# Two products taken in pieces: the pieces put between two weight slabs instead of behind both

## The chip, the cores and the metric

The kernel runs on one core of a Trainium2 chip. The metric is the time of one execution on the device, in microseconds (us). The core has five engines with an instruction stream each: TensorE (matrix products), VectorE, ScalarE, GpSimd and SyncE, which here only issues transfers. They meet at semaphores: an instruction adds to one when it is done, and another engine waits until it has reached a value.

## The reference

Two layers of a decoder (width 2048) for 512 prompt tokens and 8 samples of 4 tokens, 544 columns in all. Only the beginning of the first layer matters here:

```
def ada_norm(x, c, ada_w, ada_b, norm_g):
    mod = jax.nn.silu(c) @ ada_w + ada_b
    shift, scale, gate = jnp.split(mod, 3, axis=-1)
    h = rms_norm(x, norm_g) * (1 + scale[:, None]) + shift[:, None]
    return h, gate[:, None]

def even_layer(...):
    h, gate = ada_norm(x, c, ada_w, ada_b, norm_g)
    qa, ka, va, ga, qb, kb, vb, gb, lr = split_cols(h @ w_in, EVEN_SPLITS)
    ...
```

`shift` and `scale` are products of 9 condition vectors (one of the prompt, 8 of the samples) with a weight of 2048 x 2048 each. `h` needs both, channel by channel. `h @ w_in` sums over all 2048 channels. Window attention and gated linear attention follow, an output projection, and a second layer with retention. Everything is in float32.

## The kernel before, in words

Activations lie with channels on the 128 partitions: 16 channel tiles of 128 x 544, numbered k. A product with a block of 128 weight columns is a sum over the 16 k. To keep float32 accuracy, weights and activations are split in a high and a low part (`W_hi`, `W_lo`, `act_hi`, `act_lo`, `WH`, `WL`, `AH`, `AL` in the code), and each k takes three matmuls (high x high, high x low, low x high) for each half of 272 columns. The first two blocks, keys (ka) and values (va) of the first layer, are the "first two products". They are kept in two accumulators at once, `PJ` and the first two banks of `X`.

The shift and scale weights come in eight pairs of slabs, i = 0 to 7. Slab 0 of pair i holds 256 shift columns and slab 1 the same 256 scale columns, 2 MB each (2048 KB). There is one buffer for each kind. So SyncE (L295, `ada_slabs`) issues the slab of pair i + 1 once the semaphore `ad_done` says that TensorE has multiplied the slab of pair i of the same kind.

TensorE multiplies a slab in `ada_slab` (L1498, the matmuls 128x256): slab 0 into bank `AD`, slab 1 into bank 4 of `X`. ScalarE copies the rows out (L627), `ada_slabs_select` (L1506) turns them back into columns, and VectorE adds the bias and writes `mod_even` (L1015). Then `first_norm` on VectorE and ScalarE makes the normed and modulated activations of the two channel tiles of this pair (ending with `act_lo`, L1039 and L1042); it tells of them by the semaphores `nl` and `nls0`.

`first_products(p)` on TensorE (L1537, matmuls 128x272) adds the two channel tiles of pair p to both products: 2 tiles x 2 products x 2 halves x 3 = 24 matmuls. It waits for the norm of pair p.

The order of the work is that in which the code of each engine is written; there is no scheduler. TensorE's loop goes over i = 1 to 7: both slabs of pair i, then the selects, then pieces of the products. From i = 3 on, the pieces of pair i - 1 stand behind the selects of pair i, and at i = 3 those of pairs 0 and 1 ahead of them, because the low part of the second weight block (semaphore `lo`) is there only then. `first_products(7)` stands behind the loop. When the products are complete, ScalarE copies them out (L598, L697) and splits the next weights (L594, `split_hi`), VectorE makes their low part (L992), and the third product begins (L1481).

GpSimd issues the other transfers. Two stores of the first residual (L386, 2176 KB each, all activations as loaded) wait for `ad_ev` 14, which is VectorE's last sum of pair 6. All transfers share the same 16 transfer engines; those of SyncE are in one queue (q1), those of GpSimd in another (q0).

Of the kernel before, what the change touches and what calls it, by code (L numbers as in the profile page):

```python
# [93 lines left out]
def build(nc, I, O, C):  # L94
    ctx = ExitStack()
    with ctx:
# [129 lines left out]
        s = {}  # L226
# [1232 lines left out]
        def _(pe):  # L1459
# [29 lines left out]
            def sum_rows(lhs, src, banks=(0, 1)):  # L1489
                for c in range(2):  # L1490
                    last = mm(X[:, banks[c], 0:HALF], lhs, src[:, c * HALF:(c + 1) * HALF], start=True, stop=True)  # L1491
                return last

            def ada_rows(w, bank):

                for k in range(KT):
                    g = 32 * (k % 4)
                    last = mm(bank[g:g + 32, 0:256], cs[:, 9 * k:9 * k + 32], w[:, k], start=(k < 4), stop=(k >= KT - 4),  # L1498
                              tile_position=(0, g))
                last.then_inc(s["ad_done"], 1)  # L1500
# [18 lines left out]
            def ada_slab(i, sl):  # L1519
                if i >= 1:  # L1520
                    pe.wait_ge(s["ad_ev"], 2 * i + sl - 1)
                pe.wait_ge(adl[sl], i * 16 + 16)
                ada_rows(slab[sl], AD if sl == 0 else X[:, 4])

            def ada_slabs_select(i):
                for sl in range(2):
                    ada_select(i * 2 + (sl + 1), arow0[:, sl], AD if sl == 0 else X[:, 4])

            def first_products(p):

                pe.wait_ge(s["nls0"], p + 1)
                for k in (2 * p, 2 * p + 1):
                    pe.wait_ge(s["nl"], k + 1)
                    for n, acc in ((0, PJ), (1, X)):
                        for c in range(2):
                            for a, (w, x) in enumerate(((WH, AH), (WH, AL), (WL, AH))):
                                last = mm(acc[:, c, 0:HALF], w[:, n, k], x[:, k, c * HALF:(c + 1) * HALF],  # L1537
                                          start=(k == 0 and a == 0), stop=(k == KT - 1 and a == 2))
                            if k == KT - 1:
                                last.then_inc(s["half"], 1)  # L1540
# [13 lines left out]
            ada_slabs_select(0)  # L1554
            for i in range(1, 8):
                ada_slab(i, 0)
                ada_slab(i, 1)
                ada_slabs_select(i)
                if i == 1:
                    pe.wait_ge(s["sqd"], KT + 1)  # L1560
                    sum_rows(ones[:, :], ssum).then_inc(s["ms"], 1)
                if i == 3:
                    pe.wait_ge(s["lo"], 2)
                    first_products(0)
                    first_products(1)
                if i >= 3:
                    first_products(i - 1)
            first_products(7)
            pe.wait_ge(s["vld2"], 16 * 6)
            pe.wait_ge(s["kv_rb"], 1)  # L1570
# [363 lines left out]
```

## Time and profile before

| | |
|---|---|
| median of 3 runs | 3147.58 us (3136.74 to 3150.88) |
| profiled execution | 3144.75 us, span 3142.8 us |
| mean granted clock of TensorE | 0.955 |
| TensorE busy | 2950.2 us (94% of the span) |
| VectorE, ScalarE, GpSimd busy | 1131.0, 922.9, 238.5 us |
| read from and written to memory | 370.36 and 72.51 MB |
| matmuls of L1481, three kinds of 5920 each | 293, 290 and 289 ns in the mean |

The span goes from the first to the last instruction of one execution; busy time is the time in which an engine had at least one instruction under way. Matmuls overlap, so that a matmul of 290 ns starts some 126 ns behind the one before it. Releasers are inferred: a row says for whom an engine waited by the profile.

### The profile page before, as it was taken

The page shows a single profiled execution, that of the slowest core. Times are in us where ns is not written, and L with a number is a line of the kernel's source. Part 1 is how long each engine was busy: PE and PEld are TensorE (multiplying, and loading weights), DVE is VectorE, ACT ScalarE, POOL GpSimd, SP SyncE. Part 2 cuts the span into 40 slices and gives each one's busy share as a digit, 9 for nine tenths or more (in the row PEclk, how much of TensorE's full clock was granted, in tenths as well). Part 3 has the DMA queues.
Part 4 walks back from the last instruction along what each step waited for, and adds up shares of the span by engine and source line. Part 5 has one row for each costly group of instructions (what it writes and reads, how often), then busy time and mean ns, then how long its engine had stood idle before and what let it go on. Part 6 is the DMA issues. An engine that isn't in the chain of part 4 may idle for free.

```text
span 3142.8 us, 53302 instructions
## 1 busy us (share of the span) xinstructions
PE 2950.2 (94%) x22444; PEld 2720.7 (87%) x22444; DVE 1131.0 (36%) x1628; ACT 922.9 (29%) x1346; POOL 238.5 (8%) x381
## 2 busy tenths in 40 slices
PE   4799997988989898999999999999999999899998
PEld 3688886977878897989989898989989898799998
DVE  4334442232232434433334343333434243433422
ACT  3244443232332322223223232322323232311221
POOL 1010000000000000001010100101010010110111
PEclk8899997988989898899999999999999999999999
DMA  9953332654645343325253443435343442655442
GB/s 319 325 160 115 113 114 75 183 150 151 187 147 163 105 138 100 116 85 168 85 174 105 135 133 109 154 89 167 95 152 115 128 152 81 198 166 168 116 136 64
DMA packets 525813, 442.86 MB, mean 141 GB/s; under 512 B 12255, under 2 KB 492021, under 8 KB 525056
## 3 DMA queue, kind: packets, MB, share of 16 engines
q1 hardware_dynamic: 485664, 300.30, 33.3%
q0 software_dynamic: 39808, 139.43, 12.6%
q8 instruction: 177, 2.90, 0.4%
q14 instruction: 20, 0.16, 0.0%
q10 hardware_dynamic: 144, 0.07, 0.0%
HBM read 370.36 MB, written 72.51 MB: 141 GB/s over the span
## 4 chain that ended last, share of the span: by engine, by line
PE 84%; DMA 5%; DVE 4%; ACT 4%; issue 3%; POOL 0%; ACTq 0%; DVEq 0%; SPq 0%; POOLq 0%
PE PJ L1481 66%; DMA W_raw<-in_ada_w_even 3%; PE X L1884 2%; PE X L1463 2%; PE AD L1498 2%; PE X L1878 2%; PE X L1851 1%; PE X L1835 1%; ACT W_hi L594 1%; PE X L1826 1%; DMA work<-in_state_gla 1%; PE X L1771 1%; PE X L1498 1%; PE X L1778 1%; PE X L1491 1%
## 5 line engine op out<-in xcount | busy, mean ns | idle before, releaser
L1481 PE MATMUL PJ<-act_hi,W_hi 128*128 128x272 f32 x5920 | 1736.1, 293 | 40.4 <-DVE act_lo L1299 22.4
L1481 PE MATMUL PJ<-act_lo,W_hi 128*128 128x272 f32 x5920 | 1713.9, 290 | 0.0
L1481 PE MATMUL PJ<-act_hi,W_lo 128*128 128x272 f32 x5920 | 1712.3, 289 | 0.0
L1481 PEld LDWEIGHTS PJ<-act_hi,W_hi 128*128 128x128 f32 x5920 | 1123.9, 190 | 86.5 <-issue 64.7
L1481 PEld LDWEIGHTS PJ<-act_lo,W_hi 128*128 128x128 f32 x5920 | 1124.4, 190 | 2.8
L1481 PEld LDWEIGHTS PJ<-act_hi,W_lo 128*128 128x128 f32 x5920 | 1121.6, 189 | 0.0
L992 DVE TENSOR_TENSOR W_lo<-W_raw,W_hi 128x2048 fp32r<-128x2048 f32 x185 | 423.8, 2291 | 522.8 <-ACT W_hi L594 516.2
L594 ACT ACTIVATE W_hi<-W_raw 128x2048 fp32r<-128x2048 f32 x185 | 352.9, 1908 | 263.7 <-PE PJ L1481 244.7
L598 ACT ACTIVATE tiles<-PJ 128x272 f32<-128x272 f32 (+1 forms) x224 | 88.9, 397 | 1029.1 <-PE PJ L1481 1028.5
L1381 DVE SCALAR_TENSOR_TENSOR W_raw<-W_raw,work,X 128x512 f32<-128x512 f32 x128 | 90.0, 745 | 143.7 <-PE X L1835 143.7
L1498 PE MATMUL AD<-W_raw,cs 128*32 128x256 f32 x1280 | 90.8, 432 | 17.9 <-DMA W_raw<-in_ada_w_even 13.1
L1498 PEld LDWEIGHTS AD<-W_raw,cs 128*32 128x32 f32 x1280 | 42.2, 122 | 54.7 <-issue 33.6
L598 ACT ACTIVATE work<-PJ 128x272 f32<-128x272 f32 x50 | 19.7, 395 | 210.6 <-PE PJ L1481 205.9
L515 POOL DMA_DIRECT2D out<-W_raw x64 | 46.5, 727 | 349.0 <-DVE W_raw L1381 344.8
L1331 DVE SCALAR_TENSOR_TENSOR work<-PJ,eps,work 128x240 f32<-128x240 f32 x32 | 15.0, 468 | 159.9 <-PE PJ L1481 159.9
L1884 PEld LDWEIGHTS X<-tiles,work 128*128 128x128 f32 x256 | 46.1, 190 | 30.0 <-issue 19.2
L1884 PE MATMUL X<-tiles,work 128*128 128x512 f32 (+3 forms) x256 | 71.7, 433 | 0.0
L1463 PE MATMUL X<-ident,tiles 128*128 128x128 f32 (+1 forms) x346 | 46.4, 283 | 23.4 <-DVE tiles L1176 13.5
L1463 PEld LDWEIGHTS X<-ident,tiles 128*128 128x128 f32 (+1 forms) x346 | 38.0, 139 | 27.8 <-DVE tiles L1176 15.1
L454 POOL DMA_DIRECT2D work<-resid x48 | 26.1, 544 | 438.7 <-DVE work L1335 246.0
L1371 DVE TENSOR_TENSOR tiles<-tiles,work 128x544 f32<-128x544 f32 x32 | 23.2, 724 | 92.4 <-ACT work L610 92.4
L1878 PE MATMUL X<-work 128*128 128x512 f32 x128 | 56.2, 592 | 0.0
(341 smaller groups left out, 2159.0 us busy)
## 6 DMA issues: line engine op xcount, KB each, us to landing
W_raw<-in_w_in_odd SPq DMA_DIRECT2D x96, 1024.0 KB, 5.8
W_raw<-in_ada_w_even SPq DMA_DIRECT2D x24, 2048.0 KB, 9.7
W_raw<-in_ada_w_odd SPq DMA_DIRECT2D x24, 2048.0 KB, 8.4
W_raw<-in_w_in_even SPq DMA_DIRECT2D x40, 1024.0 KB, 11.0
W_raw<-in_state_ret POOLq DMA_DIRECT2D x64, 512.0 KB, 6.6
out<-W_raw POOLq DMA_DIRECT2D x64, 512.0 KB, 3.2
W_raw<-in_w_out_odd SPq DMA_DIRECT2D x32, 1024.0 KB, 5.9
W_raw<-in_w_out_even SPq DMA_DIRECT2D x16, 1024.0 KB, 5.8
```

The source lines that it names most:

```text
L515: pool.dma_start(O[9][0][b, ds(h, 1)].rearrange("h (k p) e -> p (h k) e", p=128), SB[:, b % 4]).then_inc(sst[b % 4], 16)
L594: A(WH[:, par], first_raw if isinstance(n, int) and n < 2 else slot[par], ACT.Copy).then_inc(s["hi"], 1)
L598: return A(dst, PJ[0:rows, c, 0:HALF], ACT.Copy).then_inc(s["ev"], 1)
L992: TT(WL[:, par], raw_w, WH[:, par].bitcast(F32), ALU.subtract).then_inc(s["lo"], 1)
L1381: STT(SB[:, b % 4, kk], SB[:, b % 4, kk], RT[:, T + NS + NB + 4:T + NS + NB + 5], X[:, kk, :], ALU.mult, ALU.add).then_inc(s["c_upv"], 1)
L1463: return nc.tensor.transpose(out, in_, ident[0:rows, 0:rows])
L1481: last = mm(PJ[:, c, 0:HALF], w[:, par, k], x[:, k, c * HALF:(c + 1) * HALF], start=(k == 0 and a == 0), stop=(k == KT - 1 and a == 2))
L1491: last = mm(X[:, banks[c], 0:HALF], lhs, src[:, c * HALF:(c + 1) * HALF], start=True, stop=True)
L1498: last = mm(bank[g:g + 32, 0:256], cs[:, 9 * k:9 * k + 32], w[:, k], start=(k < 4), stop=(k >= KT - 4), tile_position=(0, g))
L1771: last = mm(X[:, 4, NS * e + NQ * b:NS * e + NQ * b + NQ], ST[:, b, ec], BP[:, 0, SEQ + NQ * b:SEQ + NQ * b + NQ], start=False, stop=(b == ...
L1878: last = mm(X[:, kk, :], KTK[:, t, 128 * kk:128 * kk + 128], CT[:, t], start=(t == 0), stop=(t == 3))
L1884: last = mm(X[:, 2 + e % 2, 128 * t:SEQ], CT[:, t, 128 * e:128 * e + 128], RAT[:, RAOFF[t]:RAOFF[t] + SEQ - 128 * t], start=(t == 0), stop ...
```

## The change

In TensorE's loop the pieces are moved. From i = 4 on, the pieces of pair i - 1 stand between slab 0 and slab 1 of pair i. The pieces of pairs 0 to 2, which stood behind the selects of pair 3, go to the same place at i = 4, ahead of those of pair 3, together with their wait for `lo`. Only `first_products(7)` stays behind the last selects. No other engine's code is touched.

```diff
--- before.py
+++ after.py
@@ -1554,17 +1554,17 @@
             ada_slabs_select(0)
             for i in range(1, 8):
                 ada_slab(i, 0)
+                if i == 4:
+                    pe.wait_ge(s["lo"], 2)
+                    for p in range(3):
+                        first_products(p)
+                if i >= 4:
+                    first_products(i - 1)
                 ada_slab(i, 1)
                 ada_slabs_select(i)
                 if i == 1:
                     pe.wait_ge(s["sqd"], KT + 1)
                     sum_rows(ones[:, :], ssum).then_inc(s["ms"], 1)
-                if i == 3:
-                    pe.wait_ge(s["lo"], 2)
-                    first_products(0)
-                    first_products(1)
-                if i >= 3:
-                    first_products(i - 1)
             first_products(7)
             pe.wait_ge(s["vld2"], 16 * 6)
             pe.wait_ge(s["kv_rb"], 1)
```

On TensorE, behind the last select of pair 3 (`AD` and `X` with `cs` are slab products, with `sel` selects, `PJ` with `act` and `W` the first piece):

```order
 L1506 MATMUL AD<-sel,work 128x9 x2
 L1506 MATMUL X<-sel,work 128x9 x2
+L1498 MATMUL AD<-W_raw,cs 32x256 x16
 L1537 MATMUL PJ<-act_hi,W_hi 128x272
 L1537 MATMUL PJ<-act_lo,W_hi 128x272
```

The product of slab 0 of pair 4 now stands ahead of the first piece.

On TensorE, between the pieces of pair 2 and those of pair 3:

```order
 L1537 MATMUL X<-act_lo,W_hi 128x272
 L1537 MATMUL X<-act_hi,W_lo 128x272
-L1498 MATMUL AD<-W_raw,cs 32x256 x16
-L1498 MATMUL X<-W_raw,cs 32x256 x16
-L1506 MATMUL AD<-sel,work 128x9 x2
-L1506 MATMUL X<-sel,work 128x9 x2
 L1537 MATMUL PJ<-act_hi,W_hi 128x272
 L1537 MATMUL PJ<-act_lo,W_hi 128x272
```

The slabs and selects of pair 4 are gone from here, so that four calls, 96 matmuls, stand in one row.

On TensorE, between the pieces of pair 6 and those of pair 7:

```order
 L1537 MATMUL X<-act_lo,W_hi 128x272
 L1537 MATMUL X<-act_hi,W_lo 128x272
+L1498 MATMUL X<-W_raw,cs 32x256 x16
+L1506 MATMUL AD<-sel,work 128x9 x2
+L1506 MATMUL X<-sel,work 128x9 x2
 L1537 MATMUL PJ<-act_hi,W_hi 128x272
 L1537 MATMUL PJ<-act_lo,W_hi 128x272
```

Slab 1 of pair 7 and the selects now stand ahead of the last 24 pieces alone.

## Rows read from the trace of the kernel before

**Rows 1.** the page: span, clock in 40 slices, chain that ended last
```profile
span 3142.8 us, 53302 instructions
...
PEclk8899997988989898899999999999999999999999
...
PE 84%; DMA 5%; DVE 4%; ACT 4%; issue 3%; POOL 0%; ACTq 0%; DVEq 0%; SPq 0%; POOLq 0%
```

**Rows 2.** chain of waits in order of time: start, duration, what
```profile
94.44 12.74 DMA W_raw<-in_ada_w_even
...
110.93 9.08 DMA W_raw<-in_ada_w_even
...
122.96 13.92 DMA W_raw<-in_ada_w_even
...
150.23 0.78 ACT work L598 x2
...
152.26 1.81 ACT W_hi L594
...
156.44 12.31 PE PJ L1481 x96
```

**Rows 3.** timeline of TensorE: start, duration, engine, line, what [idle time before]
```profile
81.02 0.61 PE L1506 MATMUL X<-sel,work 128*128 128x9 f32 x4
...
81.70 0.29 PE L1537 MATMUL PJ<-act_lo,W_hi 128*128 128x272 f32 x1
...
90.50 0.29 PE L1537 MATMUL X<-act_hi,W_lo 128*128 128x272 f32 x1
...
101.29 3.26 PE L1498 MATMUL AD<-W_raw,cs 128*32 128x256 f32 x32 [2.67 <-DMA W_raw<-in_ada_w_even]
...
124.58 0.57 PE L1537 MATMUL PJ<-act_hi,W_hi 128*128 128x272 f32 x1
124.95 0.43 PE L1537 MATMUL PJ<-act_lo,W_hi 128*128 128x272 f32 x1
...
127.67 0.41 PE L1537 MATMUL PJ<-act_lo,W_hi 128*128 128x272 f32 x1
...
129.28 1.93 PE L1498 MATMUL AD<-W_raw,cs 128*32 128x256 f32 x32
137.01 3.64 PE L1498 MATMUL X<-W_raw,cs 128*32 128x256 f32 x32 [5.80 <-DMA W_raw<-in_ada_w_even]
```

**Rows 4.** timeline of SyncE's queue: slabs 4.0, 4.1 and 5.0 issued
```profile
76.39 0.37 SPq L295 DMA_DIRECT2D W_raw<-in_ada_w_even  x1
...
80.58 0.37 SPq L295 DMA_DIRECT2D W_raw<-in_ada_w_even  x1
...
92.72 0.37 SPq L295 DMA_DIRECT2D W_raw<-in_ada_w_even  x1
```

**Rows 5.** transfers issued at 76.39, 80.58, 92.72: size, us from issue to landing
```profile
W_raw<-in_ada_w_even SPq DMA_DIRECT2D x1, 2048.0 KB, 9.3
...
W_raw<-in_ada_w_even SPq DMA_DIRECT2D x1, 2048.0 KB, 11.1
...
W_raw<-in_ada_w_even SPq DMA_DIRECT2D x1, 2048.0 KB, 8.4
```

**Rows 6.** busy time in stretches: length, then each engine, PEclk, DMA share, GB/s
```profile
90.00:94.00 4.00, 4.00 (x70) 2.55 (x69) 0.00 (x0) 0.38 (x1) 0.00 (x0) 1.00 0.14 39
137.00:148.00 11.00, 10.99 (x65) 9.01 (x66) 5.20 (x15) 1.96 (x4) 0.73 (x2) 0.50 1.12 343
```

**Rows 7.** timeline of VectorE: last act_lo of the norms of pairs 3, 4, 7
```profile
85.62 0.22 DVE L1042 TENSOR_TENSOR act_lo<-work,act_hi 128x64 fp32r<-128x64 f32 x1
...
99.48 0.22 DVE L1042 TENSOR_TENSOR act_lo<-work,act_hi 128x64 fp32r<-128x64 f32 x1
...
146.44 0.22 DVE L1042 TENSOR_TENSOR act_lo<-work,act_hi 128x64 fp32r<-128x64 f32 x1
```

**Rows 8.** timeline of GpSimd: the two stores of the residual
```profile
125.24 1.85 POOL L386 DMA_DIRECT2D resid<-tiles  x2 [43.47 <-DVE mod_even L1015]
```

## The prediction

> **What bounds the kernel now.** I read the head of the page first. TensorE carries most of the chain that ended last, and the granted clock is near full except in the first tenth of the span [rows 1]. So an edit pays or costs only where TensorE is made to wait for something else. Next I read the chain of waits for the stretch that the change touches, about 76 to 157 us. There the chain is not TensorE's work but transfers: of the slab pairs of the shift and scale product, the second slab of pair 5 is issued at 94.44 and lands 12.74 later, that of pair 6 takes 9.08 from 110.93, that of pair 7 takes 13.92 from 122.96 [rows 2]. I write 4.0 and 4.1 for the first and the second slab of pair 4, and so on; "piece" is one of the 24 matmuls of 128x272 that a `first_products` call issues. SyncE issues 5.0 only when 4.0 has been multiplied, and 5.1 when 4.1 has. So TensorE sets the issue of each slab of the next pair, and a late slab product leaves the queue empty. That has happened once before the change: 5.0 is issued only at 92.72 [rows 4], while 4.1 landed at 80.58 + 11.1 = 91.7 [rows 4, 5], and from 90 to 94 us the transfer engines are busy 0.14 of the time [rows 6]. The cause is in TensorE's own order: 72 pieces from 81.5 to 90.7 stand ahead of slab 4.0, which had landed at 76.39 + 9.3 = 85.7 [rows 3 to 5].
>
> **Unit prices.**
> - Pieces at 2.4 GHz: 70 steps from 81.70 to 90.50, 0.1257 us each. At 1.2 GHz (granted clock 0.50, half of 2.4): 12 steps from 124.95 to 127.67, 0.2267 each [rows 3]. The run that begins at 124.58 has 14 slow pieces before the clock rises; its 24 pieces take 129.28 - 124.58 = 4.7.
> - One slab's product: 1.93 at the full clock (129.28), 3.26 after an idle time of 2.67 (101.29), 3.64 after 5.8 (137.01) [rows 3].
> - A slab issued into an empty queue lands after 8.4 (5.0: 92.72 to 101.1) [rows 4, 5]. One that queues lands about 6.06 after the slab ahead (5.1: 94.44 + 12.74 = 107.18) [rows 2]. The next two took 12.83 together (to 120.01) [rows 2].
> - From the end of a slab 1 product to the end of the norm that needs it: 99.70 - 94.44 = 5.3 after pair 4, 146.66 - 140.65 = 6.0 after pair 7 [rows 2, 3, 7]. A slab's end is when the queue issues the next (94.44), or the start and length of its product (137.01 + 3.64).
>
> **The change part by part.** It adds and removes no instruction; VectorE, ScalarE, GpSimd and SyncE keep their orders. It moves the pieces of TensorE. I walk through the pairs.
>
> Pair 4. TensorE is through with pair 3 at 81.02 + 0.61 = 81.6 [rows 3], and slab 4.0 is now next. It lands at 85.7, so TensorE, which used these 4.1 us for pieces, idles. The slab's product starts at 85.8 and takes 3.6, by the row after a like idle time: 89.4. SyncE issues 5.0 at 89.5 instead of 92.72, a gain of 3.2. It lands at 97.9, as 4.1 is out at 91.7.
>
> Now the call for pairs 0 to 2 and the one for pair 3, 96 pieces, stand between 4.0 and 4.1. No input is late: the norm of pair 3 hangs on the select that ends at 81.6 and was done at 85.62 + 0.22 = 85.8 [rows 7], now under the wait for 4.0. With 14 slow pieces, as at 124.58, they take 14 x 0.2267 + 82 x 0.1257 = 13.5, to 102.9. Slab 4.1 has lain ready since 91.7; its product ends at 104.8, and SyncE issues 5.1 at 104.9 instead of 94.44. It finds an empty queue and lands at 113.3 instead of 107.18: **+6.1**. Put as idle transfer time: 3.4 us between 4.1 and 5.0 go, 9.3 us between 5.0 and 5.1 come.
>
> This is the step on which all rests: the 96 pieces are 13.5 us, while the wait they are to fill is a slab's 6.06.
>
> Pairs 5 and 6. The queue stays full after that. 6.0 is issued at 108.0 (1.1 for the selects, an estimate from the 0.61 of one of the two in rows 3, then 1.93 and the step to the queue) while 5.1 is under way. 6.1 is issued at 115.5, behind 5.1's product. With the 12.83 of before for two slabs, 6.1 lands at 126.1 instead of 120.0, still +6.1. 6.0 lands near 119.4; its product starts after 3 us without work and ends at 122.8; then one call of 24 pieces (the norm behind it is done at 115.4 + 5.3 = 120.7) takes 4.7, to 127.5, and only then 6.1, landed 1.4 earlier, to 129.4. 7.1 is issued at 129.5 and could land at 137.9. 7.0, issued at 122.9, lands at 132.2, and 7.1 behind it at 138.2, so the 1.4 us of lateness stays hidden by 0.3. If the clock is low for 6.1 as well (3.6 for 1.93, and 5.4 for 4.7), it costs 2 us more.
>
> Pair 7. The two stores of the residual, 2176 KB each, are issued from 125.24, 2.3 behind 7.1's issue [rows 2, 8], and lengthen its way: 136.88 against 120.01 + 12.1 = 132.1, that is 4.8. The stores wait for pair 6's select, so they move along with 7.1, and I carry the 4.8 over: 143.0, +6.1. If they met less of it, up to 2 would come back.
>
> The tail. Before, 48 pieces stand behind the last select, and the norm of pair 7 ran under the first 24. Afterwards only 24 stand there, all needing that norm. From 7.1's landing: 0.14 + 3.64 + 6.0 = 9.8 to the norm's end. Then 24 pieces, at the low clock 5.4 and with the last copies 6.0 to the next weight split on ScalarE; at the full clock 15 pieces to the first copy, 1.9, and the 2.03 between ScalarE's first copy and that split as before [rows 2], 4.0 in all. So 15.8 or 13.8, against 152.26 - 136.88 = 15.4: **+0.4** or -1.6. The granted clock in the stretch of before was 0.50 from 137 to 148, though TensorE was busy for 10.99 of those 11 us [rows 6], so I take the low one. The saving of 24 pieces behind the last slab is thus spent on a norm that nothing covers any more.
>
> From there nothing is new: the first matmul on the loaded weights started at 156.44, behind copy, split and remainder [rows 2], and the whole queue shifts. The sum is 6.1 + 0.4 = **+6.5 us**. Against the profiled execution (3144.75, span 3142.8) that gives 3151.3. The median of the runs lies 2.8 above it, so against that, 3147.6 + 6.5 = **3154**.
>
> Bounds of the unknown, the clock in the new order: if it never falls, 4.0 and 4.1 cost 1.93 each and the 96 pieces 12.1: 5.1 is issued at 101.9, +3.1, and with the fast tail +1.5. If it stays low through all of it, see the third rival.
>
> The trace shows a slab alone at 8.4. The Trainium skill's page "DMA: Bandwidth & Descriptors", section "Anatomy of one DMA — SWDGE (gpsimd) path", fits 2.0 us plus bytes over 436 GB/s to one transfer of GpSimd's path, which for 2 MB is an estimate of 6.8 us and 4.8 per further slab. By it 5.1 would land at 111.7, and the delay would be near +4.5. These are SyncE's transfers and the rows have them slower, so the measured steps stand.
>
> **Rivals.**
> 1. Faster: the queue never runs empty, and the tail is short. The 3.4 us of idle transfer time [rows 6] go and the tail is -1.6: -5.0, 3142.6. For it: 5.0 does go out 3.2 earlier. Against it: 4.1's product would have to be done by about 95.5, so 96 pieces in 4 us; at 0.1257 they need 12. It could come in part if the pieces or transfers run otherwise than I read. Chance 0.12.
> 2. No shift: the delay is swallowed by something later that comes at a fixed time; 3147.6. For it: loads of the next weights are issued behind 7.0 and do not wait for the pieces. Against it: ScalarE's split, VectorE's remainder and the matmul at 156.44 follow one another without a gap [rows 2]. Chance 0.10.
> 3. Slower beyond doubt: TensorE's clock stays at 1.2 GHz once it has waited for 4.0, through the 96 pieces and on. Its price: 82 x 0.101 = 8.3 and 1.7 for slab 4.1, then the 2.0 of pair 6: 6.5 + 12.0 = +18.5, 3166. It decides from the point where nearly all 96 pieces are slow; each one costs 0.1. For it: 11 us at 0.50 under full work [rows 6]. Against it: that needs some 25 us; the run at 124.58 was out of it after 14 pieces. Chance 0.10. The Trainium skill speaks for this rival: "TensorE: Matmul & The Clock Gate", section "Loop structure matters more than you think", wants matmuls back to back and calls waits for transfers between their groups the way to a cold engine, and the change puts each group between two such waits. The trace agrees in part: the pieces at 124.58 and those up to 148 ran slow, those from 81.70 on did not [rows 3, 6].
>
> The forecast has 0.63; 0.05 is left for what I don't see.
>
> **How the numbers follow.** About 0.5%, 15.7 us, is what a measurement of this kernel can tell from no change. Forecast and the first two rivals lie within it; only the third crosses it, and just so, as does part of the rest: slower 0.06, faster 0.02, the same 0.92. The runs of before themselves lie from 3136.7 to 3150.9. The range runs from a little below the first rival to the third: 3141 to 3167. The forecast's own, without a run's scatter, is 3149 to 3157.
>
> **What would show it.** Slab 5.0 issued near 89.5 and 5.1 near 105; 96 pieces in one row between the two slab products; transfer engines idle for 7 to 10 us from about 98, and busy from 90 to 94; 7.1 landing near 143; 24 pieces behind the last norm, with VectorE's last act_lo ahead of them; the first matmul of the third product near 163. It is wrong if 5.1 is issued before 100, if the engines show no such hole, or if the third product starts no later than 156.4.

## The result, and the profile after

| | before | changed |
|---|---|---|
| median, 21 runs each | 3145.48 us | 3149.08 us |
| range | 3136.74 to 3153.41 | 3147.60 to 3153.01 |
| ratio of the runs | | 1.0016, 95% interval 1.0009 to 1.0024 |
| profiled execution, span | 3144.75, 3142.8 | 3147.86, 3145.9 |

In microseconds the ratio is +5.0, between +2.8 and +7.5. It is taken over all runs; the two medians alone are 3.6 apart. The forecast was 3154, +6.5. The 3154 stood on a median of before over 3 runs, which lies 2.1 above that over 21, so the shift is what can be compared.

The chain of waits of the changed kernel, in order of time (start, duration, what), answers to [rows 2]:

```profile
76.15 9.38 DMA W_raw<-in_ada_w_even
...
106.41 12.22 DMA W_raw<-in_ada_w_even
...
127.39 17.82 DMA W_raw<-in_ada_w_even
...
145.34 3.64 PE X L1498 x32
...
159.53 0.41 ACT work L598
...
161.18 1.91 ACT W_hi L594
...
165.46 4.55 PE PJ L1481 x34
```

The chain now runs over first slabs: 4.0 (issued at 76.15) and 6.0 (106.41), and only at the end over 7.1, whose way is 17.82 us instead of 13.92. The third product starts at 165.46 instead of 156.44, 9.0 later.

TensorE's timeline (start, duration, engine, line, what [idle time before]), against [rows 3]:

```profile
85.67 3.47 PE L1498 MATMUL AD<-W_raw,cs 128*32 128x256 f32 x32 [2.43 <-DMA W_raw<-in_ada_w_even]
89.06 0.49 PE L1537 MATMUL PJ<-act_hi,W_hi 128*128 128x272 f32 x1
89.40 0.29 PE L1537 MATMUL PJ<-act_lo,W_hi 128*128 128x272 f32 x1
...
101.22 0.29 PE L1537 MATMUL X<-act_hi,W_lo 128*128 128x272 f32 x1
101.44 1.93 PE L1498 MATMUL X<-W_raw,cs 128*32 128x256 f32 x32
...
145.34 3.64 PE L1498 MATMUL X<-W_raw,cs 128*32 128x256 f32 x32 [8.04 <-DMA W_raw<-in_ada_w_even]
...
155.04 0.60 PE L1537 MATMUL PJ<-act_hi,W_hi 128*128 128x272 f32 x1 [4.25 <-DVE act_lo L1042]
...
160.43 0.43 PE L1537 MATMUL X<-act_hi,W_lo 128*128 128x272 f32 x1
```

Slab 4.0, then 96 pieces from 89.06 to 101.4 in one row, then 4.1. Only the first piece is slow. At the end 7.1's product starts at 145.34 after 8.04 us of waiting, and the last 24 pieces wait 4.25 us for the norm and then go in steps of 0.23: (160.43 - 155.04) / 23.

SyncE's queue, slabs 5.0, 5.1 and 7.1, and under it their way from issue to landing, against [rows 4, 5]:

```profile
89.17 0.37 SPq L295 DMA_DIRECT2D W_raw<-in_ada_w_even  x1
...
103.43 0.37 SPq L295 DMA_DIRECT2D W_raw<-in_ada_w_even  x1
...
127.39 0.37 SPq L295 DMA_DIRECT2D W_raw<-in_ada_w_even  x1
```
```profile
W_raw<-in_ada_w_even SPq DMA_DIRECT2D x1, 2048.0 KB, 8.1
...
W_raw<-in_ada_w_even SPq DMA_DIRECT2D x1, 2048.0 KB, 8.2
...
W_raw<-in_ada_w_even SPq DMA_DIRECT2D x1, 2048.0 KB, 17.8
```

5.0 goes out 3.6 us earlier than before, 5.1 goes out 9.0 later. Between them the engines rest. Busy time in stretches (length, engines, granted clock, share and GB/s of the transfers), against [rows 6]:

```profile
97.00:104.00 7.00, 7.00 (x73) 5.87 (x73) 0.05 (x1) 0.38 (x1) 0.00 (x0) 1.00 0.00 0
90.00:94.00 4.00, 4.00 (x34) 4.00 (x33) 0.00 (x0) 0.00 (x0) 0.00 (x0) 1.00 0.96 318
146.00:158.00 12.00, 7.75 (x49) 5.89 (x42) 5.34 (x15) 1.95 (x4) 2.40 (x5) 0.50 1.02 286
```

From 97 to 104 us nothing is moved at all; the hole of before at 90 to 94 is filled (0.96). Behind slab 7.1, from 146 to 158 us, TensorE's granted clock is 0.50. VectorE's last act_lo of pair 7 and the stores, against [rows 7, 8]:

```profile
154.77 0.22 DVE L1042 TENSOR_TENSOR act_lo<-work,act_hi 128x64 fp32r<-128x64 f32 x1
...
128.95 1.85 POOL L386 DMA_DIRECT2D resid<-tiles  x2 [47.05 <-DVE mod_even L1015]
```

### The profile page after: what moved, and what is told of

It reads as the page before. It is cut to its first block, busy times and chain, and to the rows that moved or that the text cites. A ratio compares the mean times of both kernels' runs of the same rounds, so it can differ in the third digit from the quotient of the medians.

```text
span 3145.9 us, 53302 instructions
## 1 busy us (share of the span) xinstructions
PE 2947.7 (94%) x22444; PEld 2718.0 (86%) x22444; DVE 1130.9 (36%) x1628; ACT 923.0 (29%) x1346; POOL 238.5 (8%) x381
## 4 chain that ended last, share of the span: by engine, by line
PE 84%; DVE 5%; DMA 4%; ACT 4%; issue 3%; POOL 0%; ACTq 0%; DVEq 0%; POOLq 0%; SPq 0%
PE PJ L1481 65%; PE AD L1498 2%; PE X L1884 2%; DMA W_raw<-in_ada_w_even 2%; PE X L1463 2%; PE X L1878 2%; PE X L1851 1%; PE X L1835 1%; ACT W_hi L594 1%; PE X L1826 1%; DMA work<-in_state_gla 1%; PE X L1491 1%; PE X L1778 1%; PE X L1771 1%; PE X L1622 1%
## 5 line engine op out<-in xcount | busy, mean ns | idle before, releaser
L598 ACT ACTIVATE work<-PJ 128x272 f32<-128x272 f32 x50 | 19.7, 395 | 209.8 <-PE PJ L1481 204.5
L1463 PE MATMUL X<-ident,tiles 128*128 128x128 f32 (+1 forms) x346 | 46.4, 283 | 23.4 <-DVE tiles L1176 13.5
```

The costliest lines, as they stand in the source:

```text
L598: return A(dst, PJ[0:rows, c, 0:HALF], ACT.Copy).then_inc(s["ev"], 1)
L1463: return nc.tensor.transpose(out, in_, ident[0:rows, 0:rows])
```

## The experiments

All twelve kernels, the ratio of their runs to those of the kernel before on the same chip, and four times of each one's profile. The times of a profile are of one execution. "7.1's way" is from issue to landing.

| kernel | ratio to before (95%) | 5.1 issued | 6.1 lands | 7.1's way | third product |
|---|---|---|---|---|---|
| before | | 94.4 | 120.0 | 13.9 | 156.4 |
| before, again | 0.9994 (0.9984 to 1.0004) | 98.5 | 123.7 | 14.9 | 159.0 |
| changed | 1.0016 (1.0009 to 1.0024) | 103.4 | 124.6 | 17.8 | 165.5 |
| changed, again | 1.0025 (1.0014 to 1.0037) | 103.4 | 124.5 | 18.3 | 165.4 |
| two calls between 4.0 and 4.1 | 1.0008 (0.9999 to 1.0018) | 97.5 | 118.7 | 17.2 | 159.1 |
| one call between | 1.0019 (1.0008 to 1.0029) | 97.8 | 120.0 | 19.9 | 163.1 |
| spread | 0.9980 (0.9970 to 0.9989) | 95.7 | 117.9 | 17.8 | 156.1 |
| before, stores issued with 7.1 | 1.0017 (1.0007 to 1.0027) | 96.9 | 122.4 | 20.7 | 164.2 |
| changed, stores behind 7.1 | 1.0004 (0.9993 to 1.0016) | 104.1 | 125.1 | 9.5 | 158.2 |
| before, stores behind 7.0 | 0.9994 (0.9984 to 1.0004) | 96.7 | 122.3 | 9.3 | 150.3 |
| changed, stores behind 7.0 | 0.9987 (0.9977 to 0.9998) | 103.1 | 124.1 | 9.6 | 154.5 |
| one call, stores behind 7.0 | 0.9990 (0.9980 to 1.0001) | 99.6 | 122.2 | 10.3 | 153.3 |
| spread, stores behind 7.0 | 0.9967 (0.9957 to 0.9977) | 94.2 | 115.9 | 9.5 | 145.3 |
| changed, pair 6 behind the last select | 1.0008 (0.9995 to 1.0022) | 103.6 | 124.7 | 18.5 | 163.8 |

**One call between the slabs.** Theory A is the prediction's: the 96 pieces empty the queue. The code excerpts here and below are set against the changed kernel, unless another is named; lines between those shown are left out.

```diff
                 ada_slab(i, 0)
-                if i == 4:
-                    pe.wait_ge(s["lo"], 2)
-                    for p in range(3):
-                        first_products(p)
                 if i >= 4:
                     first_products(i - 1)
                 ada_slab(i, 1)
                 ada_slabs_select(i)
+                if i == 3:
+                    pe.wait_ge(s["lo"], 2)
+                    for p in range(3):
+                        first_products(p)
```

> Only one part of the change: one call of pieces (24) between the two slabs from pair 4 on, while the three calls of pairs 0 to 2 stay behind the select of pair 3, as before. Theory A (the 96 pieces between 4.0 and 4.1 empty the transfer queue): 5.0 is issued at 92.7 as before, 5.1 near 97.7, which still queues behind 5.0, so 7.1 lands at 137 +- 1.5 and the third product's first matmul starts at 157 +- 2 instead of 156.44; time within 0.1% of before. Rival B (any pieces between two slabs delay the second slab or cost the clock): 7.1 at 141 or later and the third product at 161 or later, 0.15% or more slower than before.

5.1 was issued at 97.8 and 6.1 landed at 120.0, as in before: with 24 pieces there is no new hole. But the third product started at 163.1 and the kernel was 0.19% slower, and both are B's numbers. Most of the loss came in one piece, at 7.1: 19.9 us on its way, though issued at 122.93 as before. So A was right about the hole, the hole was not the whole loss, and B was not yet out. Something lengthened 7.1's way.

**Spread.** Never more than one call between two slab products.

```diff
                 ada_slab(i, 0)
                 if i >= 4:
-                    first_products(i - 1)
+                    first_products(2 * i - 7 if i < 6 else i - 2)
                 ada_slab(i, 1)
                 ada_slabs_select(i)
+                if i in (3, 4):
+                    first_products(2 * i - 6)
+                if i == 7:
+                    first_products(6)
```

(The batch at i = 4 is gone, the wait for `lo` stands at i = 3.)

> The eight calls are spread so that never more than one stands between two slab products: pair 0 behind the select of pair 3, 1 between 4.0 and 4.1, 2 behind the select of pair 4, 3 between 5.0 and 5.1, 4 between 6.0 and 6.1, 5 between 7.0 and 7.1, 6 and 7 behind the last select. Theory A: 5.0 is issued near 88 to 89.5, 5.1 near 94 to 95.5, no hole in the transfers between 90 and 130 us, 7.1 lands 3 us or more ahead of before's 136.88 (133), the third product starts near 153, and the time is 0.1% below before and 0.25% below the changed kernel. Rival B (pieces between slabs cost by themselves): no earlier than before, third product at 157 or later.

6.1 landed at 117.9 and the kernel is the first that is faster than before. In its own profile the third product, at 156.1 and not near the 153 expected, is only 0.3 us ahead of before's first profile, since 7.1 again took 17.8 instead of 13.9 and landed at 138.6. That profile is of the slowest of its 12 runs, and its slab 3.1 took 3.64 us at 78 us, as in before's second profile (see "Before again"). Against that one the third product is 2.9 us ahead.

**Stores behind 7.1.** One more wait of GpSimd ahead of the two stores.

```diff
             pool.wait_ge(s["ad_ev"], 14)
+            pool.wait_ge(s["ad_done"], 16)
```

> The changed kernel, with the two residual stores waiting for slab 7.1's product besides. Theory C (in the changed kernel 7.1's landing is late by two causes: 4.7 us from the queue's hole and 3.7 us more from meeting the stores): 7.1 lands one slab behind 7.0, at 136 to 137.5 instead of 145.2, and the third product starts at 157 +- 2 instead of 165.46. Rival D (the stores do not matter, the 17.8 us way of 7.1 is the queue's): 7.1 lands at 143 or later. If the stores come in the way of the norm's end or of the next weights instead, 7.1 is early and the third product is not.

Rival D is out: 7.1's way fell from 17.8 to 9.5 us. It landed at 138.4, 0.9 behind the expected range. The third product came 7.2 earlier, at 158.2, within its range, though VectorE now stood 8.68 us for the first store (its timeline):

```profile
154.65 0.59 DVE L1109 MEMSET tiles<- 128x640 f32 x1 [8.68 <-DMA resid<-tiles]
```

**The changed kernel again.**

> The changed kernel once more, unaltered. It tells whether the 9.0 us that the first profile shows at the third product, and their decay to 3.1 at the end in steps of 1.5, come again. If the delay at the third product is fixed and the later steps are chance (the clock's phase), the third product starts at 165 +- 1 and the steps stand elsewhere; if later waits swallow it, the same steps stand at the same places.

The third product started at 165.4. Against the first profile of before the delay then stood at 11.6 at 371 us, 8.3 at 828, 7.3 at 1083 and 6.2 at the end; the first profile of changed had 9.0, 7.1, 4.7 and 3.1 there. In both the changes come in steps, most of them near 1.5 us and partly at the same places. The first half of the expectation holds, the second in part: "Before again" shows where several of these steps belong.

**Stores behind 7.0.** `ad_ev` 14 is replaced by `ad_done` 15, so that the stores start to move when 7.1 is almost in. The excerpt is set against before.

```diff
-            pool.wait_ge(s["ad_ev"], 14)
+            pool.wait_ge(s["ad_done"], 15)
```

> The kernel before, with the two residual stores waiting for the product of slab 7.0 instead of the modulation of pair 6, so that they move bytes about 5 us after it, when 7.1 is almost in. Theory C (what is left of 7.1 when the stores begin goes at a fifth of its rate): 7.1 lands 6.1 behind 7.0, near 132, instead of 136.9, and the third product starts near 151.7 instead of 156.4; the time is 0.1 to 0.2% lower. Rival D: 7.1 lands at 136 or later, nothing changes.

> The changed kernel with the same later stores. Theory A + C: 5.1 is issued near 103.4, 7.0 lands near 130.5, 7.1 near 136.7 instead of 145.2, the third product starts near 157 instead of 165.4. Against the kernel before with the same stores that leaves 4.7 to 5.3 us, the queue's hole alone, 0.15 to 0.17%. If the hole had cost nothing by itself (all of it by the stores), both would start the third product at the same time.

> One call of pieces between the slabs (pairs 0 to 2 behind the select of pair 3 as before), with the later stores. In the first run of this arrangement 6.1 landed at 120.0 as before, but 7.1 took 19.9 us. Theory A + C: 7.1 lands 6.1 behind 7.0, at 133, third product near 153.4, within 2 us of the kernel before with later stores. Rival B (pieces between slabs cost by themselves): third product at 157 or later.

> The spread calls with the later stores; the version that the reasons so far point to. Theory A + C: 7.1 lands at 130 to 131 instead of 138.5, the third product starts at 148 +- 1.5, 8 us ahead of the kernel before; time 0.2 to 0.35% below before. It falls short if the next weight load or the first store's landing now holds the third product.

In all four 7.1 landed 6.0 to 7.3 behind 7.0, in 9.3 to 10.3 us. With one call between the slabs the third product started at 153.3 and not at 157 or later, so rival B is out too; it was 3.0 behind before's, not within 2. In before, 7.1 landed at 134.5 and not near 132, and the whole time did not fall by the 0.1 to 0.2% expected. In the spread order the third product came at 145.3, earlier than expected.

With the stores away, the changed order starts the third product 4.2 later than before's, one call 3.0 later, spread 5.0 earlier. Of the 4.2 of the changed order, 2.2 lie in the landing of 7.1 (136.65 against 134.46), so the hole by itself costs less than the 4.7 to 5.3 expected, though before's own landings were late in this profile (6.1 at 122.3 and not 120.0, see "Before again"). The other 2.0 lie behind it: from 7.1's landing to the third product it takes 17.9 and 18.0 us in the two kernels that have only 24 pieces behind the last select, and 15.8 in the two that have 48. In the whole time, before and changed with these stores can't be told apart: 0.9994 and 0.9987, intervals overlapping. So what the new order costs with the stores away is shown at the third product, not in the whole time.

Before gained 6.1 at the third product and had 0.8 of it left at 194 us, because the stores now met the load of the next weights. That load as issued, its way, and what the engines waited for from 150 to 180 us:

```profile
134.26 0.83 SPq L269 DMA_DIRECT2D W_raw<-in_w_in_even  x1
```
```profile
W_raw<-in_w_in_even SPq DMA_DIRECT2D x1, 1024.0 KB, 20.5
```
```profile
ACT W_hi L594 <- DMA W_raw<-in_w_in_even: 14.6, 2, 7.7
```

The load took 20.5 us; in before the same one took 15.8. Spread with these stores is the fastest kernel, 0.33% under before; its transfers do not rest in the two stretches in which the others have their holes:

```profile
90.00:94.00 4.00, 3.23 (x44) 2.38 (x42) 0.00 (x0) 0.00 (x0) 0.00 (x0) 1.00 1.09 348
97.00:104.00 7.00, 6.47 (x68) 5.17 (x66) 2.41 (x7) 1.69 (x4) 0.00 (x0) 1.00 1.09 347
```

**Stores earlier.** The sharpest test of the stores: TensorE's order is that of before, the stores are issued with 7.1 (`ad_done` 14 instead of `ad_ev` 14), 0.3 us behind it instead of 2.3.

> The kernel before, its two residual stores issued 2.3 us earlier, with slab 7.1 itself. TensorE's order is untouched. Theory C (once the stores move, the slab queue gets a fifth of its rate, so what counts is how long 7.1 has run alone): the stores begin to move near 128 instead of 130.4, 7.1 has run alone for some 2 us instead of 4.4, and lands near 142 instead of 136.9, with the second store; third product near 161.5 instead of 156.4; 0.1 to 0.2% slower. Rival D (the length of 7.1's way in the changed kernel comes from pieces or the hole, not from the stores): 7.1 lands within 1.5 us of 136.9.

7.1 took 20.7 us and the kernel became 0.17% slower, as much as by the change itself. It landed at 146.0 and the third product started at 164.2, both later than expected: 7.1 ran alone for 1.7 us, from the landing of 7.0 at 128.3 to the stores' first packet at 130.0. Packets, MB and time of both queues in 134 to 136 us, first of this kernel, then of before:

```profile
q0 software_dynamic: 154, 0.67, 80.9%
q1 hardware_dynamic: 156, 0.16, 22.4%
```
```profile
q0 software_dynamic: 189, 0.81, 98.2%
q1 hardware_dynamic: 109, 0.02, 5.4%
```

Here is the mechanism. While both queues have work, each sends as many packets (154 and 156), but a packet of the stores carries 4.4 KB (0.67 MB in 154) and one of the slab 1 KB. From 132 to 140 us the counts are 630 and 626. The slab queue moves 0.16 MB in 2 us; alone it moved 1.28 MB in 4 us before:

```profile
q1 hardware_dynamic: 1253, 1.28, 101.3%
```

That is 320 KB per us alone against 80 beside the stores. In before, 7.1 ran alone from 126.0 until the stores' first packet at 129.8, so at 134 hardly any of it was left (0.02 MB in 2 us). No run changed the size of the packets; that it is their size which sets the shares is read from these counts. The Trainium skill's page "DMA: Bandwidth & Descriptors", section "Queues, rings and completion order", says that an engine goes round the queues packet by packet. The packet counts of this trace agree as far as they go. The page's packet is a group of descriptors, and no row here tells how many of the profile's packets make one.

**Pair 6 behind the last select.**

```diff
-                if i >= 4:
+                if 4 <= i < 7:
                     first_products(i - 1)
                 ada_slab(i, 1)
                 ada_slabs_select(i)
+                if i == 7:
+                    first_products(6)
```

> The changed kernel, with the pieces of pair 6 put back behind the last select. The tail's step of the prediction: the norm of pair 7 takes what the 24 pieces fewer would save, so the third product starts at the same time (165.4 +- 1), 7.1 lands as before at 145.5 +- 0.7. Rival: fewer pieces behind the last slab do help, and the third product starts 2.5 us or more later than in the changed kernel.

Neither expectation held. 7.1 landed at 146.1, and from there the third product was 17.6 us away, against 20.2 and 19.7 in the two profiles of changed. So the 24 pieces moved ahead cost 2 to 2.6 us here. This kernel's windows behind its last select:

```profile
150.00:154.00 4.00, 4.00 (x32) 4.00 (x32) 2.86 (x10) 1.81 (x4) 0.00 (x0) 0.97 1.15 324
154.00:158.00 4.00, 2.86 (x23) 2.64 (x22) 2.48 (x6) 0.59 (x3) 2.09 (x4) 1.00 1.11 350
```

The granted clock is 0.97 and 1.00, and TensorE rests 1.14 us ahead of the last 24 pieces. In the changed kernel it rests 4.25 us there, and the last 24 go in steps of 0.23 at a granted clock of 0.50.

**Two calls.**

> A middle dose: the calls of pairs 0 and 1 behind the select of pair 3, those of pairs 2 and 3 between 4.0 and 4.1 (48 pieces on either side). Theory A: slab 4.0's product ends near 89.5 after 48 pieces, 5.1 is issued near 97.5 and lands near 106, between the 107.1 of one call and before and the 111.6 of the changed kernel and ahead of both; transfers at rest for about 2 us. Later landings follow it: 6.1 near 118.5. What the stores do to 7.1 then depends on its lead on them; with 1.5 us between their issue it has no more time alone than in the changed kernel, and takes 17 us or more. Rival B: 6.1 lands at 122 or later.

5.1 at 97.5, landing at 105.8, 6.1 at 118.7, 7.1's way 17.2: all as expected. 48 pieces leave the transfers at rest for about 2 us (shares 0.44 and 0.63 from 96 to 98 and 98 to 100 us), less than the hole of before; 96 leave 7.

**Before again.**

> The kernel before once more, unaltered. Third product at 156.5 +- 1.5, 7.1 landing 13.9 +- 1 after its issue. Of the delays against the first profile of before, steps of about 1.5 us in both directions are expected between 300 us and the end, as between the two profiles of the changed kernel; they are what makes the whole time scatter.

The third product started at 159.0, outside what was expected by 1.0; the steps of 1 to 1.5 us are there (5.7 at 310 us, 1.3 at 664, 2.1 at 1083, 1.2 at the end). Those near 375, 1461 and 2185 us stand in the two profiles of changed as well, so they are the first profile's own. Against this second profile of before, the second of changed is 6.4 late at the third product, 4.9 at 194 us, 5.2 at 1083 and 5.0 at the end. The difference between the two profiles of before is made at 78 us. Slab 3.1's product, of the first profile of before and of this one:

```profile
78.60 1.94 PE L1498 MATMUL X<-W_raw,cs 128*32 128x256 f32 x32 [2.26 <-DMA W_raw<-in_ada_w_even]
```
```profile
78.53 3.64 PE L1498 MATMUL X<-W_raw,cs 128*32 128x256 f32 x32 [2.26 <-DMA W_raw<-in_ada_w_even]
```

The granted clock from 80 to 84 us was 1.00 in the first and 0.50 in this one. Where it is low there, the 72 pieces begin late and slow (the first at 83.8 instead of 81.5), and everything up to pair 5 is 2.3 to 4 us later (5.1 issued at 96.7, 96.9 and 98.5 in three profiles with before's order, whose slab 3.1 took 3.41, 2.58 and 3.64). Why the clock is low there in one execution and not in another, no row shows. In the changed order nothing comes of it: TensorE waits for 4.0 anyway, and 5.1 was issued between 103.1 and 104.1 in five profiles. The first profile of before was a fast one, so that 9.0 us overstates the loss.

## Why the prediction was right, and where its sizes were off

| step | forecast | changed kernel |
|---|---|---|
| 5.0 issued | 89.5 | 89.2 |
| 96 pieces | 13.5 | 12.4 |
| 5.1 issued, landed | 104.9, 113.3 | 103.4, 111.6 |
| 6.1 landed, against before | 126.1, +6.1 | 124.6, +4.6 |
| 7.1 landed | 143.0, +6.1 | 145.2, +8.3 |
| third product against before's profile | +6.5 | +9.0 |
| whole | +6.5 | +5.0 (2.8 to 7.5) |

**What bounds the stretch** was read rightly: transfers, whose issue TensorE sets by the slab product ahead. Moving 96 pieces between 4.0 and 4.1 sends 5.0 out 3.6 us earlier and 5.1 9 us later, and the hole is 7 us in the windows.

**The clock in the pieces.** I took 14 slow ones, and one was slow: 1.1 us too much in the pieces. Rival 3 (everything slow, +18.5) did not come in any of these profiles; its case is the tail alone.

**Carrying the 4.8 us of the stores over** is the step that was mis-sized. 7.1 would have landed at 130.6 + 6.06 = 136.7 and came at 145.2: 8.5. I had written that the stores move along with 7.1. They do, by the select, but what counts is how long 7.1 runs alone. In before 7.0 is in at 126.0 and the stores' first packet moves at 129.8: 3.8 us of lead. In the changed kernel 7.0 is in at 130.6, and the stores, issued only 1.6 instead of 2.3 behind 7.1, move from 133.5: 2.9 us (3.2 in its second profile). From that first packet to the landing of 7.1, 129.82 to 136.87 in before and 133.49 to 145.21 in the changed kernel, the queues moved (packets, MB, time):

```profile
q0 software_dynamic: 584, 2.49, 85.9%
q1 hardware_dynamic: 501, 0.32, 16.0%
```
```profile
q0 software_dynamic: 940, 4.02, 83.2%
q1 hardware_dynamic: 1158, 0.70, 20.3%
```

Nearly all MB of q1 are slab 7.1's. So 0.38 MB more of it was left when the stores came. At 80 KB per us, an estimate from the rows under "Stores earlier", that is 4.7 us, less 0.9 of shorter lead: 3.8, against the 3.7 that were missing. Of the 0.38 MB, 0.28 follow from the lead (0.9 us at 320 KB per us); the other 0.1 I can't place. That the stores do it is shown from both sides, by the earlier stores and by the kernels with later ones.

**The tail** was forecast at 15.8 us from 7.1's landing to the weight split (+0.4). It was 161.18 - 145.2 = 16.0 (+0.6). The step holds against the first profile of before, and by luck: in that profile the granted clock was 0.50 up to 148 us, under the last slab's product and some 24 of the 48 pieces. From 7.1's landing to the third product it took 19.6 us, while the four other profiles with 48 pieces there and the stores beside 7.1 took 17.5 to 18.2, and the four with 24 pieces 19.7 to 20.3. So the tail costs about 2 us, not 0.4, and my reason, that the fewer pieces' gain is spent on the norm, was too kind to the change.

**From the stage to the end.** The prediction took the shift one for one. By mean landings, before (four profiles with its order up to pair 6) has 6.1 at 122.1 and changed (five) at 124.6, +2.5. From there to 7.1 it is 16.9 and 17.6 against 20.6, 21.2 and 21.5, +3.9. From 7.1 to the third product it is 19.6 and 17.6 against 20.2 and 19.7, +1.3. Together +7.7, just above the first interval and within the second one (1.0014 to 1.0037, +4.4 to +11.6). So the forecast of +6.5 was near, with a hole less than half as dear as I wrote, and the stores and the tail dearer. That these errors nearly cancel is luck; what was right is the hole, its place and its cause. How much of the shift is swallowed later stays open: between the two second profiles 1.4 of the 6.4 us are gone by the end, and the steps of 1.5 us, which also stand between two executions of the same kernel, hide the rest.

**Rivals.** The first (faster, the queue never empty) failed for the reason given, and is what the spread order makes true. The second (no shift) is excluded by the interval.

## What to carry to other kernels

Work moved into a wait holds nothing back up to about the length of the wait: 24 pieces between two slabs made no new hole in the transfers and 48 one of about 2 us, 96 made one of 7 us, and the same pieces spread one call at a time gave 0.2% instead of costing 0.16%. That does not make the move free: with the stores where they were, the kernel with 24 pieces there was 0.19% slower, by 7.1's way and the tail. Look at what the moved work holds back, not only at what it fills. When the slabs' transfer of 1 KB packets met the stores' of 4.4 KB, the slab crawled, so the time at which the neighbouring transfer starts is worth as much care as the slab's own: with the pieces spread and the stores later, the kernel is 0.33% faster than before.

## What the runs showed that I had not expected

- Two queues shared by packets, not bytes (154 and 156 in 2 us), and the queue with the small ones fell to a quarter of its speed.
- From their issue to their first packet the stores took 4.4 to 4.9 us in ten profiles, and 1.7 to 2.1 us in the four with the stores behind 7.0. No run shows why.
- Between two profiles of one kernel the place of an instruction near 1083 us differs by 2.1 us (before) and 2.6 us (changed), in steps near 1.5, while the runs of before and of before again agree to 0.06%.
- The same slab product took 1.94 or 3.64 us at 78 us in two executions of the same code, and the third product started 2.6 us later in the execution with the slow one.
